# Moving half of the weight residuals of a two-model float32 stack from VectorE to GpSimd

## What is computed

```python
def first_block(x, c, ctx, ...):
    for l in range(2):
        sa, ca, ga, sm, cm, gm = ada_params(c, w_ada[l], b_ada[l])
        h = modulate(rms_norm(x, g_mix[l]), sa, ca)
        u, q, k, v = split_heads(h @ w_in[l])
        mix = concatenate([pool_mixer(u), head_out(diff_attn(rope(q), rope(k), v))])
        x = x + ga * (mix @ w_out[l])
        x = x + gm * (square(relu(modulate(rms_norm(x, g_mlp[l]), sm, cm) @ w_mlp1[l])) @ w_mlp2[l])
    return rms_norm(x, g_final)

def second_block(x, ...):
    for l in range(2):
        hn = rms_norm(h, mix_norm_g[l])
        h = h + (even_mixer(hn) if l == 0 else odd_mixer(hn))
        h = h + conv_ffn(rms_norm(h, ffn_norm_g[l]))
    return rms_norm(h, final_norm_g)
```

## Time and profile before

| | |
|---|---|
| median of 3 runs | 1806.52 us (1805.97 to 1809.26) |
| profiled execution | span 1805.1 us from its first to its last instruction; no other time of that execution is listed |
| TensorE busy | 1651.4 us, 91% |
| VectorE busy | 1176.8 us, 65%, in 1708 instructions |
| ScalarE busy | 831.3 us, 46% |
| GpSimd busy | 4.6 us, in 13 instructions |
| `split_lo`, line 1216 | 476 instructions, 573.9 us |
| `split_hi`, line 831 | 476 instructions, 491.3 us |
| TensorE's mean granted clock | 0.944 |

### The profile page before, as it was taken

The page is one execution under the profiler, slowest core; times in us unless marked ns, Lnnn a source line. Parts: engine busy times, 40 slices in busy tenths (PEclk is TensorE's granted clock), DMA queues, the critical chain, the costliest instruction groups (busy, mean ns, idle before and its releaser), DMA issues.

```text
span 1805.1 us, 27935 instructions
## 1 busy us (share of the span) xinstructions
PE 1651.4 (91%) x11302; PEld 1487.6 (82%) x11302; DVE 1176.8 (65%) x1708; ACT 831.3 (46%) x1151; POOL 4.6 (0%) x13
## 2 busy tenths in 40 slices
PE   6899898999999997998899979957999998899997
PEld 4787576888888886786899978947999988899997
DVE  6854856645444556766666668685767777876775
ACT  6323733424232333245444444423655556665553
POOL 0000000000000000000000000000000000000000
PEclk8999988999999998999899989958999999899998
DMA  8433034333333332550455543402455544445451
GB/s 357 168 140 140 1 116 164 140 117 125 134 136 139 129 129 91 187 187 24 140 179 177 181 152 116 142 24 89 145 186 186 179 147 164 140 141 186 168 197 53
DMA packets 35561, 258.03 MB, mean 143 GB/s; under 512 B 3968, under 2 KB 3984, under 8 KB 4512
## 3 DMA queue, kind: packets, MB, share of 16 engines
q1 hardware_dynamic: 34704, 253.06, 39.7%
q0 software_dynamic: 784, 3.95, 0.6%
HBM read 255.95 MB, written 1.05 MB: 142 GB/s over the span
## 4 chain that ended last, share of the span: by engine, by line
PE 80%; DVE 13%; ACT 3%; issue 2%; DMA 1%; SPq 0%; DVEq 0%; ACTq 0%
PE ps L379 18%; PE ps L380 17%; PE ps L381 17%; PE ps L399 4%; PE ps L400 4%; PE ps L401 4%; PE ps L467 3%; DVE w_lo L1216 3%; PE ps L450 2%; PE ps L451 2%; PE ps L452 2%; PE ps L487 2%; DVE small L1340 1%; ACT w_hi L831 1%; DVE wgt L1357 1%
## 5 line engine op out<-in xcount | busy, mean ns | idle before, releaser
L831 ACT ACTIVATE w_hi<-w_raw 128x1024 fp32r<-128x1024 f32 x476 | 491.3, 1053 | 505.3 <-PE ps L381 286.7
L1216 DVE TENSOR_TENSOR w_lo<-w_raw,w_hi 128x1024 fp32r<-128x1024 f32 x476 | 573.9, 1221 | 221.0 <-ACT w_hi L831 217.7
L379 PE MATMUL ps<-h_hi,w_hi 128*128 128x256 f32 (+1 forms) x1712 | 542.2, 317 | 33.7 <-DVE h_lo L1264 16.0
L380 PE MATMUL ps<-h_lo,w_hi 128*128 128x256 f32 (+1 forms) x1712 | 538.2, 314 | 0.0
L381 PE MATMUL ps<-h_hi,w_lo 128*128 128x256 f32 (+1 forms) x1712 | 537.7, 314 | 0.0
L379 PEld LDWEIGHTS ps<-h_hi,w_hi 128*128 128x128 f32 x1712 | 335.8, 196 | 60.6 <-issue 32.9
L381 PEld LDWEIGHTS ps<-h_hi,w_lo 128*128 128x128 f32 x1712 | 335.2, 196 | 17.4
L380 PEld LDWEIGHTS ps<-h_lo,w_hi 128*128 128x128 f32 x1712 | 336.1, 196 | 16.0
L379 PE MATMUL ps<-g_hi,w_hi 128*128 128x256 f32 (+1 forms) x448 | 140.8, 314 | 0.0
L381 PE MATMUL ps<-g_hi,w_lo 128*128 128x256 f32 (+1 forms) x448 | 140.4, 313 | 0.0
L400 PE MATMUL ps<-g_lo,w_hi 128*128 128x256 f32 (+1 forms) x448 | 140.4, 313 | 0.0
(11 more groups left out here) (269 smaller groups left out, 2232.5 us busy)
## 6 DMA issues: line engine op xcount, KB each, us to landing
w_raw<-in_w_stream SPq DMA_DIRECT2D x238, 1024.0 KB, 5.0
x<-in_x_in SPq DMA_DIRECT2D x1, 2048.0 KB, 11.4
pmat<-in_pool_mats POOLq DMA_DIRECT2D x2, 1024.0 KB, 7.0
out<-y_out SPq DMA_DIRECT2D x1, 1024.0 KB, 3.9
cst<-in_cst_in POOLq DMA_DIRECT2D x1, 708.0 KB, 9.1
wp<-in_w_pool POOLq DMA_DIRECT2D x1, 512.0 KB, 5.3
gmask<-in_gla_masks POOLq DMA_DIRECT2D x1, 512.0 KB, 4.2
vec<-in_vec_in SPq DMA_DIRECT2D x1, 332.0 KB, 3.0
```

Source lines behind the costliest of these rows:

```text
L379: mm(o, wh, hi[:, k, cols], start=(k == 0), stop=False)
L380: mm(o, wh, lo[:, k, cols], start=False, stop=False)
L831: A(w_hi[:, n % 2, k, :].rearrange("p k n -> p (k n)"), w_raw[:, n % 4, k.start * CH:k.stop * CH], ACT.Copy)\
L1216: TT(w_lo[:, n % 2, k, :].rearrange("p k n -> p (k n)"), w_raw[:, n % 4, k.start * CH:k.stop * CH], w_hi[:, n % 2, k, :].rearrange("p k n ...
```

## The change

VectorE keeps the low part of the first half of each chunk. GpSimd makes the low part of the second half, for all 238 chunks in one loop, as soon as `hi_ready` tells that ScalarE has written the high part. It raises `lo_ready`, for which TensorE waits as before. SyncE now waits for both signals before it overwrites a slot of `w_raw`. GpSimd's DMAs stand between its subtractions, before chunks 9, 85, 137 and 138.

```diff
@@ sync
                 sp.wait_ge(lo_ready, n - 3)
+                sp.wait_ge(half_lo, n - 3)
                 sp.dma_start(w_raw[:, n % 4, :], w_stream[n]).then_inc(raw_in[n % 4], 16)
@@ gpsimd
+            def second_lo(n, at=None):
+                pool.wait_ge(hi_ready, n + 1 if at is None else at + 1)
+                nc.gpsimd.tensor_tensor(w_lo[:, n % 2, KT // 2:KT, :].rearrange("p k n -> p (k n)"),
+                                        w_raw[:, n % 4, KT // 2 * CH:KT * CH],
+                                        w_hi[:, n % 2, KT // 2:KT, :].rearrange("p k n -> p (k n)").bitcast(F32),
+                                        ALU.subtract).then_inc(lo_ready, 1)
+
+            for n in range(N_CHUNKS):
+                if n == 9:
+                    pool.wait_ge(half_hi, 9)
+                    pool.dma_start(wp[:, :, :, :], w_pool).then_inc(pool_in, 16)
+                    pool.dma_start(pmat[:, :, :, :], pool_mats).then_inc(pool_in, 16)
...
+                second_lo(n)
@@ vector, split_lo
-                for part in parts:
-                    dve.wait_ge((half_hi, hi_ready)[part], at(n + 1))
-                    k = slice(part * KT // 2, (part + 1) * KT // 2)
-                    TT(w_lo[:, n % 2, k, :].rearrange("p k n -> p (k n)"), w_raw[:, n % 4, k.start * CH:k.stop * CH],
-                       w_hi[:, n % 2, k, :].rearrange("p k n -> p (k n)").bitcast(F32), ALU.subtract)\
-                        .then_inc((half_lo, lo_ready)[part], 1)
+                if 0 in parts:
+                    dve.wait_ge(half_hi, at(n + 1))
+                    TT(w_lo[:, n % 2, 0:KT // 2, :].rearrange("p k n -> p (k n)"), w_raw[:, n % 4, 0:KT // 2 * CH],
+                       w_hi[:, n % 2, 0:KT // 2, :].rearrange("p k n -> p (k n)").bitcast(F32), ALU.subtract)\
+                        .then_inc(half_lo, 1)
```

More of the change, by code:

```diff
@@ L324, in _ @@
                     sp.wait_ge(lo_ready, it * 4 + (r - 3))
+                    sp.wait_ge(half_lo, it * 4 + (r - 3))
                     sp.dma_start(w_raw[:, r, :], w_stream[bass.ds(it * 4 + r, 1)].rearrange("a p n -> p (a n)"))\
@@ L338, in _ @@
             pool.dma_start(cst[:, :], cst_in).then_inc(cst_in_s, 16)
[L339 to L348, removed]
+            def second_lo(n, at=None):
[9 more added lines that the diff above has]
+                    pool.dma_start(pmat[:, :, :, :], pool_mats).then_inc(pool_in, 16)
+                if n == N_WIN[1] + 1:
+                    pool.wait_ge(psum_free, N_WIN[1])
+                    pool.dma_start(pmat[:, :, :, :], pool_mats).then_inc(pool_in, 16)
+                if n == N_EV + 1:
+                    pool.wait_ge(psum_free, N_EV)
+                    pool.dma_start(wgk[:, :, :], w_gk).then_inc(gk_in, 16)
+                    pool.dma_start(wgk2[:, :], w_gk2).then_inc(gk_in, 16)
+                if n == N_EV + 2:
+                    pool.wait_ge(rbc_ready, 6)
+                    pool.dma_start(gmask[:, :, :], gla_masks).then_inc(glam_in, 16)
+                second_lo(n)
         @block.tensor
```

## The result

The change makes the kernel slower by 0.44%: the ratio to the kernel before is 1.0044, 95% interval 1.0029 to 1.0059. The median of 6 runs is 1816.89 us (1812.66 to 1819.93) against 1807.78 us (6 runs, 1805.97 to 1809.26), so 8 to 9 us more. I had forecast 1805.9 us, no change to speak of. The time lies inside the range that I gave (1790 to 1826), but it moved where I expected it to stand.

A forecast was written before the change was run, and what follows sets the result against it. The prediction took TensorE as the bound, busy for 91% of the span and holding 80% of the chain. Its gains and losses summed to a gain of 0.6 us, hence 1805.9 us, with a range of 1790 to 1826.

The forecast's parts named there:

- the recurrence: Recurrence: `xr_lo`, for which TensorE waits, meets GpSimd's chunk 198, up to 2.1 us late, plus an earlier meeting; 2.5 us lost.
- even mixer and GLA: a loss of 1.1 us: Even mixer and GLA: a 0.71 us wait goes, but a late half costs 0.95 and the differences lose 0.9.
- The price of a subtraction on GpSimd: Every second half: a GpSimd subtraction takes 2.12 us against VectorE's 1.22, between bounds of 1.06 and 3.2 us.
- Do the engines disturb each other?: In SBUF: two-input VectorE work and a GpSimd subtraction exclude each other, one waiting up to 2.12 us; PSUM-input work is undisturbed.
- Saturated stages: nothing: MLPs and FFNs: GpSimd's half arrives in time, 3.02 us of room against 2.20 at the tightest; no change.
- In-projections: a gain of 7.8 us: Value tiles behind the rope: TensorE's stops shrink, gaining 6.2 us, and 1.6 us more from avoiding the lower clock.
- Four tile chunks, 0.8 us: Four later tile chunks of the in-projections: each has 0.2 us too little room, 0.8 us lost together.
- Entries to attention: a gain of 2.2 us: Before attention's scores: two subtractions leave VectorE's path in each layer, less 1.1 us of waiting; 2.2 us gained.
- Start: a loss of 0.5 us: Before the first norm: two subtractions leave VectorE, but the norm's diagonal and both first halves queue behind GpSimd; 0.5 us lost.
- Out-projection of layer 0: a loss of 3.5 us: Short ada chunks: GpSimd's half 0.7 to 0.8 us late four times, plus waiting by first halves; 3.5 us lost.
- The free case: Rival, whole kernel: the engines do not disturb each other, a gain of 13.2 us to 1793.3 us; chance 0.27.
- The slow case: Rival, whole kernel: a subtraction of 3.2 us or more makes TensorE wait; 1824 us with waiting, 1811 if free; chance 0.27.

The follow-up runs named there:

- `v_meet`: Kernel before, with only five second halves (chunks 148, 149, 190, 198, 199) given to GpSimd; 1812.72 us, ratio 1.0030.
- `d_copy`: Kernel before, all second halves on VectorE, plus 238 idle GpSimd copies of 128x896 that nobody reads; 1818.39 us, ratio 1.0054.
- `v_sat`: Kernel before, with GpSimd making second halves only for the MLP and FFN chunks; 1807.31 us, ratio 0.9998.
- `v_best`: Kernel before, with GpSimd making seven second halves: 16, 86, 92 behind a rope and 24, 25, 100, 101 ahead of attention; 1795.40 us, ratio 0.9927.
- `v_inp`: Kernel before, with GpSimd making only the second halves of chunks 16, 86 and 92, behind a rope; 1800.80 us, ratio 0.9961.
- `v_out0`: Kernel before, with GpSimd making only second halves 26 to 37, out-projection of layer 0 and the norm behind it; 1811.72 us, ratio 1.0020.

## Why the prediction was wrong

**The step that failed is the recurrence, "a loss of 2.5 us", and with it "even mixer and GLA: a loss of 1.1 us".** Measured alone they cost 6.1 us (3.4 to 8.9) and 4.2 us (2.0 to 6.3), together 10.3 in place of 3.6 us. In the trace of the change chunks 190 to 200 take 5.3 us more. The mechanism, mutual exclusion, was the one that I took. I applied it too narrowly, in two ways, and missed a late half. First, I let it hold up only VectorE work with two SBUF inputs. A `TENSOR_SCALAR` with one was held for 2.38 us, so that the polynomial of the odd mixer, 0.17 us an instruction, costs 2.2 us; in the step on the recurrence it does not occur. Had it been another instruction of that chain, as in `v_meet`, it would have been one with two inputs: I did not look at the chain at all, since each of its instructions is short. Second, I counted one and a half meetings in the recurrence. The trace has `w_lo`, a scan and `xr_lo`, held for 2.2, 2.1 and 1.7 us. The one that I had named, `xr_lo` on 128x1024, is not among them: it took 1.22 us again; the `xr_lo` that was held is a later one on 128x512. In the GLA I weighed the differences at 1174.74 with a wait of 0.9 us. They took 2.80 us for 0.75, and `gq` ahead of them lost 1.6 us, which I had not priced. The late half is that of chunk 142, which needs both halves at its start: I priced this for 1164.02, where the wait of 0.76 grew to 1.93 us, nearly as I said, but not for 1124.26, where 2.72 grew to 4.43.

The other steps:

- **The price of a subtraction on GpSimd.** I took 2.12 us. It is 2.41 us (median; 2.33 at least). The Trainium skill, "GPSIMD Engine Reference", section Elementwise, gives 1.96 times VectorE's time for a two-input operation: the medians of the trace agree, 2407 over 1227 ns. I had said what that would cost, 5 us more. With it the forecast would have been 1811, slower by just over 0.2%.
- **Do the engines disturb each other?** Yes, as taken. I limited it to two SBUF inputs on VectorE's side, and the Trainium skill, "SBUF — State Buffer", section Who interferes with whom, says more: a VectorE copy or `tensor_scalar` from SBUF to SBUF can contend with GpSimd too. The trace agrees (2.38 us on 128x8; 0.92 us for the copy of 128x64 in `d_copy`). I had read out of that page only the rule for two inputs. That work with a PSUM input stays undisturbed was right.
- **Saturated stages: nothing.** Right: -0.4 us (-2.4 to 1.8) in `v_sat`, and 50.00 of 50.
- **In-projections: a gain of 7.8 us.** Right in mechanism and nearly in size. The stop of 2.85 us is now 0.34 us (I said 0.2), and three chunks alone give 7.1 us (4.9 to 9.2). In the change the two rope stretches give 6.1 us of it.
- **Four tile chunks, 0.8 us** cost 2.1 us in the table, as each half is 0.3 us later than I took.
- **Entries to attention: a gain of 2.2 us.** The traces show 3.0 us, no more than these stretches vary by themselves. With these four chunks handed over beside the three it is 6 us, the difference of `v_best` and `v_inp`.
- **Start: a loss of 0.5 us.** 2.0 us (0.4 to 3.8); 1.4 in the trace of the change. The three instructions that I had named, the diagonal and two first halves, were held up, each by 1.6 to 2.0 us. I had not seen two subtractions of 128x1 that took 2.33 and 2.14 us for 0.15, nor that TensorE waits 1.0 to 1.1 us for GpSimd's half at four modulation chunks. Which of them makes the difference is not shown.
- **Out-projection of layer 0: a loss of 3.5 us.** Right: 3.6 us (1.6 to 5.6), with four waits of 0.8; the traces of `v_out0` and of the change have 2.6 and 2.7 between the same places.
- **Norms: a loss of 1.0 us.** No kernel has the norms alone. `h_lo` was held up by 0.3 us in three of them; I had it 0.35 late at one.
- **The rivals.** The free case is out. The slow case, over 3.0 us, is out for the subtraction by itself. GpSimd's queue cost next to nothing: chunk 9 alone was begun late, 1.1 us, behind two DMA issues. (The view of this queue ahead of the prediction ends early: 101 subtractions and two DMAs follow its last row.)

In sum the terms that I had at -0.5, -3.5, -1.1 and -2.5, together 7.6 us, are 15.9 us when measured one by one. The way from a gain of 0.6 to a loss of 8 us is about this difference, though each of the four is known to some 2 us only, and two of them hold a norm priced elsewhere.

## What to carry to other kernels

GpSimd as a helper beside a VectorE that works on SBUF took 290 us of work from it here and gave 205 back in holds. The bill comes in two places: where the helper's longer instruction arrives late, and where a chain of short dependent VectorE instructions is on the path. Before work goes to GpSimd, mark those chains, whatever their instructions cost, and count up to one whole GpSimd instruction for each meeting; five meetings that held VectorE for 10 us cost 5.4. If the gain stands at a few places, try the order on the first engine, and then hand over those places alone: here the order by itself gained 9 us, seven halves out of 238 gained 13, and all 238 lost 8.

## What the runs showed of the hardware

- An idle GpSimd subtraction of 128x896 per chunk (median 2.43 us) slowed this kernel by 78 us, an idle copy (median 1.24 us) by 10 us. Both only read SBUF and write a tile that nobody uses. That the longer one costs eight times as much was not expected. Part of it is that more is held up: 186 of the 476 `w_lo` last over 1.5 us beside the subtraction and 70 beside the copy, and all of them together lose 270 and 49 us. Why a duration twice as long holds up so much more stays open.
- A scan with two SBUF inputs is held up (2.80 us for 0.67), and a `TENSOR_SCALAR` of 8 columns for as long as a subtraction of 1024. Copies out of PSUM were not: the 48 copies of `rows` take 413 ns on the mean after the change, with no instance over 0.42 us.
- The lower clock after a wait differs between executions. After the same wait of 2.7 us the kernel before went on at 1.00 and `v_sat` at 0.50. The same stretch, chunks 138 to 144, took 45.1 to 48.3 us in kernels that did not touch it, so a single trace is no measure for a loss of 3 us there.
